# Up weights of an expert: column pieces of one pass in place of quarters of the rows

## The reference

```python
logits = t @ router_w + router_b              # 640 tokens x 32 experts
vals, idx = lax.top_k(logits, 4)              # 4 experts a token, softmax weights
def expert_block(e, toks, w):
    hh = t[toks] @ w_up[e] + b_up[e]          # w_up[e]: 1024 x 2048
    glu = minimum(hh[:, :1024], 7)
    lin = clip(hh[:, 1024:], -7, 7)
    y = (glu * sigmoid(1.702 * glu) * (lin + 1)) @ w_down[e] + b_down[e]   # 1024 x 1024
    return y * w
```

## Time and profile before

| | us |
|---|---|
| timed runs (three) | 1877.72, 1878.63, 1874.29; median 1877.72 |
| the profiled execution's own time | 1864.97 |
| its span, from the first to the last instruction | 1863.1 |
| PE busy with matmuls in the span | 1654.8 (89%) |
| DVE, ACT, POOL busy | 757.7, 342.3, 205.2 |

### The profile page before, as it was taken

The page is one execution under the profiler, slowest core; times in us unless marked ns, Lnnn a source line. Parts: engine busy times, 40 slices in busy tenths (PEclk is TensorE's granted clock), DMA queues, the critical chain, the costliest instruction groups (busy, mean ns, idle before and its releaser), DMA issues.

```text
span 1863.1 us, 52100 instructions
## 1 busy us (share of the span) xinstructions
PE 1654.8 (89%) x21067; PEld 988.3 (53%) x21068; DVE 757.7 (41%) x2254; ACT 342.3 (18%) x679; POOL 205.2 (11%) x274
## 2 busy tenths in 40 slices
PE   4999998987899873998998999999899998999967
PEld 2545456466675552655554565565455554555523
DVE  2432337346552666433333343334243333343317
ACT  0002211532010110221221222122122221122200
POOL 0000010200001210010110111011001100001026
PEclk9999999999899875998999999999999999999968
DMA  9634041920756256899889978998999999999994
GB/s 350 244 117 169 1 123 50 304 64 1 200 167 154 104 226 249 338 417 414 329 339 416 378 294 356 416 364 340 418 408 419 416 416 417 415 417 417 418 348 147
DMA packets 170599, 539.36 MB, mean 289 GB/s; under 512 B 24810, under 2 KB 75182, under 8 KB 137732
## 3 DMA queue, kind: packets, MB, share of 16 engines
q1 hardware_dynamic: 144080, 501.34, 69.5%
q0 software_dynamic: 7392, 22.81, 3.3%
q10 hardware_dynamic: 19028, 13.77, 2.4%
HBM read 502.57 MB, written 35.17 MB: 289 GB/s over the span
## 4 chain that ended last, share of the span: by engine, by line
PE 38%; DMA 16%; SPq 4%; DVE 1%; issue 1%; ACT 0%; POOLq 0%; POOL 0%; DVEq 0%
PE psum L1914 24%; DMA arena<-in_w_down 15%; PE psum L1922 12%; SPq L1825 3%; PE psum L1745 1%; DMA arena<-in_ln_b 1%; SPq L1830 1%; PE psum L1733 1%; SPq L1862 0%; DMA arena<-d_u,arena 0%; DVE arena L1782 0%; SPq L129 0%; DVE arena L1774 0%; SPq L131 0%; DVE arena L1776 0%
## 5 line engine op out<-in xcount | busy, mean ns | idle before, releaser
L1914 PE MATMUL psum<-arena 128*32 128x192 f32 (+1 forms) x11904 | 676.9, 385 | 53.4 <-issue 27.7
L1914 PEld LDWEIGHTS psum<-arena 128*32 128x32 f32 x11904 | 395.8, 111 | 330.7 <-issue 69.2
L1922 PE MATMUL psum<-arena 128*32 128x256 f32 x5952 | 343.3, 381 | 14.5 <-DMA arena<-in_w_down 14.5
L1975 DVE STREAM_TRANSPOSE arena<-psum 128x320 f32<-128x320 f32 (+1 forms) x186 | 83.7, 450 | 561.4 <-PE psum L1914 561.4
L1922 PEld LDWEIGHTS psum<-arena 128*32 128x32 f32 x5952 | 183.1, 110 | 147.0 <-DVE arena L1988 33.0
L1897 ACT ACT_TABLE_LOAD x93 | 119.3, 1283 | 259.8 <-issue 226.1
L1897 ACT ACTIVATE arena<-arena 128x160 f32<-128x160 f32 (+1 forms) x186 | 57.6, 310 | 401.4 <-DVE arena L1980 401.4
L428 PE MATMUL psum<-arena 128*128 128x512 f32 (+1 forms) x320 | 115.1, 521 | 0.6 <-DMA arena<-in_w_in 0.6
L1873 POOL COPY arena<-arena 128x1 uint32 (+1 forms) x94 | 17.1, 182 | 891.0 <-DVE arena L1969 852.7
L1876 POOL DMA_INDIRECT arena<-d_u,arena x94 | 92.1, 979 | 74.0 <-POOL arena L1873 74.0
L428 PEld LDWEIGHTS psum<-arena 128*128 128x128 f32 x320 | 56.9, 190 | 58.9 <-issue 57.3
(11 more groups left out here) (383 smaller groups left out, 1424.7 us busy)
## 6 DMA issues: line engine op xcount, KB each, us to landing
arena<-in_w_up SPq DMA_DIRECT2D x128, 2048.0 KB, 19.6
arena<-in_w_down SPq DMA_DIRECT2D x64, 2048.0 KB, 30.6
arena<-in_w_ada SPq DMA_DIRECT2D x10, 2048.0 KB, 19.4
d_y<-arena ACTq DMA_DIRECT2D x372, 32.0 KB, 5.8
arena<-in_w_in SPq DMA_DIRECT2D x5, 2048.0 KB, 7.7
d_y<-arena SPq DMA_DIRECT2D x1, 10240.0 KB, 33.0
arena<-in_cache_ckv SPq DMA_DIRECT2D x8, 1024.0 KB, 6.0
arena<-d_q SPq DMA_DIRECT2D x32, 144.0 KB, 3.4
```

The source lines that it names most:

```text
L1914: ins = pe.matmul(S[h][c * U:(c + 1) * U, 0:2 * U * (b1 - b0)].rearrange("p (g b j) -> p g b j", g=2, j=U), xT[:, 2 * q + k, :], up[par][q ...
L1922: ins = pe.matmul(Y[c * U:(c + 1) * U, 0:256], hidT[:, n, :], down[par][n // 4][:, n % 4, c * 256:(c + 1) * 256], start=(n == 0), stop=(n ...
L1975: dve.transpose(wide, S[h][:, 0:2 * U * w]).then_inc(s["h_turned"], 1)
```

## The change

w_up is cut in four pieces another way: by the columns of one pass and half of the rows. Pieces 0 and 1 are columns 0 to 639 of both halves g, rows 0 to 511 and 512 to 1023 (2.62 MB each); pieces 2 and 3 are columns 640 to 1023 of both halves, the same rows (1.57 MB each). The up pass goes through pieces 0, 1, 2, 3, waits for each at its own place and counts up_done after each; up_acc is dropped, and DVE waits for the second count of up_done in its place. A piece is read by two DMAs, one for each half g, whose runs of contiguous memory are 640 or 384 floats in place of 2048; a piece's semaphore then rises by 32. The sizes of the pieces ask for other addresses in the ring, and the first loads take the pieces in another order. w_down, the number of matmuls, their columns and the order over the rows within a pass stay as they are.

```diff
-RING_AT = [[43960, 48056, 15288, 11192, 19384, 23480], [31672, 27576, 3000, 7096, 35768, 39864]]
+RING_AT = [[43960, 11192, 49080, 16312, 19384, 23480], [27576, 3000, 32696, 8120, 35768, 39864]]
...
+def up_pieces(I):
+
+    rows = I["w_up"][0].rearrange("e (i k p) (g n) -> e i p k g n", i=2, p=P, g=2)
+    return [rows[:, i, :, :, :, b0 * P:b1 * P] for b0, b1 in PARTS for i in range(2)]
+
+
+def up_place(v, par, q):
+
+    b0, b1 = PARTS[q // 2]
+    return v.cut(RING_AT[par][q], 4, 2, P * (b1 - b0))
...
             def first(q):
-                sp.dma_start(v.cut(RING_AT[1][q], 2, 2 * FF), first_up(0, q)).then_inc(s["ring_in"][6 + q], 16)
-
-            first(0)
+                for g in range(2):
+                    sp.dma_start(up_place(v, 1, q)[:, :, g], w_up[q][0, :, :, g]).then_inc(s["ring_in"][6 + q], 16)
+
+            first(2)
             for t in range(NT):
                 if t == NT - 2:
                     sp.wait_ge(s["mT_acc"], 2 * NT)
-                    first(1)
+                    first(0)
                 if t == NT - 1:
                     sp.wait_ge(s["wo_acc"], NT)
-                    first(2)
+                    first(1)
                     first(3)
...
-            for q in range(3):
-                sp.dma_start(v.cut(RING_AT[0][q], 2, 2 * FF),
-                             w_up[bass.ds(long0, 1), :, q].rearrange("e p k n -> p (e k) n")
-                             ).then_inc(s["ring_in"][q], 16)
+            for q in (0, 2, 3):
+                for g in range(2):
+                    sp.dma_start(up_place(v, 0, q)[:, :, g], w_up[q][bass.ds(long0, 1), :, :, g].rearrange(
+                        "e p k n -> p (e k) n")).then_inc(s["ring_in"][q], 16)
...
             def load_up(e, par, q):
-                sp.dma_start(v.cut(RING_AT[par][q], 2, 2 * FF),
-                             w_up[bass.ds(e, 1), :, q].rearrange("e p k n -> p (e k) n")
-                             ).then_inc(s["ring_in"][6 * par + q], 16)
+                for g in range(2):
+                    sp.dma_start(up_place(v, par, q)[:, :, g], w_up[q][bass.ds(e, 1), :, :, g].rearrange(
+                        "e p k n -> p (e k) n")).then_inc(s["ring_in"][6 * par + q], 16)
...
-            load_up(long0, 0, 3)
+            load_up(long0, 0, 1)
...
-            def up_step(par, q, h):
-                b0, b1 = PARTS[h]
-                for k in range(2):
+            def up_step(par, q):
+                h, i = q // 2, q % 2
+                w = PARTS[h][1] - PARTS[h][0]
+                for k in range(4):
                     for c in range(C4):
-                        ins = pe.matmul(S[h][c * U:(c + 1) * U, 0:2 * U * (b1 - b0)
-                                             ].rearrange("p (g b j) -> p g b j", g=2, j=U),
-                                        xT[:, 2 * q + k, :], up[par][q][:, k, :, b0:b1, c, :],
-                                        start=(q == 0 and k == 0), stop=(q == 3 and k == 1))
+                        ins = pe.matmul(S[h][c * U:(c + 1) * U, 0:2 * U * w].rearrange("p (g b j) -> p g b j", g=2, j=U),
+                                        xT[:, 4 * i + k, :], up[par][q][:, k, :, :, c, :],
+                                        start=(i == 0 and k == 0), stop=(i == 1 and k == 3))
                 return ins
...
-                    pe.wait_ge(s["ring_in"][6 * par + g], times * 16 + RING_USED[6 * par + g])
+                    pe.wait_ge(s["ring_in"][6 * par + g], times * (32 if g < 4 else 16) + RING_USED[6 * par + g])
...
-                for h in range(NPART):
-                    for q in range(4):
-                        if h == 0:
-                            loaded(q)
-                        ins = up_step(par, q, h)
-                        if h == NPART - 1:
-                            ins.then_inc(s["up_done"], 1)
-                    if h < NPART - 1:
-                        ins.then_inc(s["up_acc"], 1)
+                for q in range(4):
+                    loaded(q)
+                    up_step(par, q).then_inc(s["up_done"], 1)
...
-                                dve.wait_ge(s["up_acc"], b * (NPART - 1) + (1 + h))
+                                dve.wait_ge(s["up_done"], b * 4 + 5)
```

More of the change, by code:

```diff
@@ L1374, in _ @@
             sp.dma_start(raw, I["b_up"][0].rearrange("e (q k p) -> (e q) k p", q=4, p=P)).then_inc(s["rw_in"], 16)
-            first_up = lambda e, q: I["w_up"][0, e].rearrange("(q k p) n -> q p k n", k=2, p=P)[q]
+            w_up = up_pieces(I)
             first_down = lambda e, h: I["w_down"][0, e].rearrange("(h n p) d -> h p n d", h=2, p=P)[h]
             def first(q):
-                sp.dma_start(v.cut(RING_AT[1][q], 2, 2 * FF), first_up(0, q)).then_inc(s["ring_in"][6 + q], 16)
-            first(0)
+                for g in range(2):
+                    sp.dma_start(up_place(v, 1, q)[:, :, g], w_up[q][0, :, :, g]).then_inc(s["ring_in"][6 + q], 16)
+            first(2)
             for t in range(NT):
@@ L1401, in _ @@
             long0 = sp.value_load(v.order[0:1, 0:1], min_val=0, max_val=NE - 1)
-            w_up = I["w_up"][0].rearrange("e (q k p) n -> e p q k n", k=2, p=P)
-            for q in range(3):
-                sp.dma_start(v.cut(RING_AT[0][q], 2, 2 * FF),
-                             w_up[bass.ds(long0, 1), :, q].rearrange("e p k n -> p (e k) n")
-                             ).then_inc(s["ring_in"][q], 16)
+            for q in (0, 2, 3):
+                for g in range(2):
+                    sp.dma_start(up_place(v, 0, q)[:, :, g], w_up[q][bass.ds(long0, 1), :, :, g].rearrange(
+                        "e p k n -> p (e k) n")).then_inc(s["ring_in"][q], 16)
         @block.scalar
@@ L1795, in stage_experts @@
     C4 = 4
-    up = [[v.cut(RING_AT[par][q], 2, 2, FF).rearrange("p k g (b c j) -> p k g b c j", b=KD, c=C4) for q in range(4)]
-          for par in range(2)]
+    up = [[v.cut(RING_AT[par][2 * h + i], 4, 2, P * (b1 - b0)).rearrange("p k g (b c j) -> p k g b c j", b=b1 - b0, c=C4)
+           for h, (b0, b1) in enumerate(PARTS) for i in range(2)] for par in range(2)]
     down = [[v.cut(RING_AT[par][4 + h], 4, D) for h in range(2)] for par in range(2)]
@@ L2025 @@
 top_neg ex_ready wts_ready hot_ready hot_acc sc2_ready mask_ready pos_acc order_ready idx_in idx_seen xg_in xT_ready bias_acc bias_set bias_sel
-up_acc up_done down_done h_turned h_sum h_clip h_cut h_prod sig_ready hid_ready
+up_done down_done h_turned h_sum h_clip h_cut h_prod sig_ready hid_ready
 y_ready y_out ohw_turned ohwT_ready f_in
```

## The result

The changed kernel takes 1905.8 us in the median of four runs (1899.22 to 1910.47) against 1877.76 of the kernel before (four runs): the medians lie 28.0 us (1.5%) apart. The ratio of the runs with its 95% interval is 1.0170 (1.0138 to 1.0201), which is 26 to 38 us. The profiled execution took 1904.67 us (span 1902.8).

A forecast was written before the change was run, and what follows sets the result against it. The prediction saw an expert stage bound by PE in its middle and by DMA elsewhere, above all from 1267 us on. Terms +2.8 and +26.8 make +29.6 us: 1877.7 + 29.6 = 1907 us, range 1884 to 1924 us.

The forecast's parts named there:

- Two regimes: Expert stage: with many tokens per expert transfers wait for PE; with two or three units left PE waits for transfers.
- the two busy runs: Expert stage, DMA busy throughout: three loads from 788.31 us, +2.8 us; 16 loads from 1267.45 us, +26.8 us.
- The price of a run: w_up loads: shorter contiguous runs make each expert's load 1.85 us longer, bounds 0 and 4.2 us.
- the line through four rates: Rates of 4 KB, 2 KB, 1 KB and 512 B rows give 37 ns per KB and about 9.5 ns per row.
- The release: Expert's last unit: the first transfer can start 2.80 us earlier, counted once in each of two DMA-busy stretches.
- Everything else at zero. PE: PE in the expert stage: 64 matmuls a unit, same columns in the same order of k, so no cost.
- Matmul means are unchanged: Sign that the forecast is right: the mean time of PE's matmuls stays as before.
- SP at zero: SP's queue: 8 issues for 4 per load, 0.65 us apart, cost nothing since SP waits 477.5 us for PE.
- Free runs: Rival for the stretch from 1267 us: short runs cost nothing, -5.6 us, 1872 us; chance 0.10.
- half the price: Rival on w_up loads: 0.85 us a load in place of 1.85, +10.6 us, 1888 us; chance 0.12.
- the price of the 1 KB row: Rival on w_up loads: short reads go like 1 KB rows, 4.2 us more a load, +74 us, 1952 us; chance 0.05.
- holes swallow the rest: Rival for the last DMA-busy stretch: PE sets the pace and DMA's idle time covers the price, about 1878 us; chance 0.05.

The follow-up runs named there:

- one factor: Changed kernel with each half of w_down also read by two transfers, so every weight semaphore rises by 32: 1.0150 to the kernel before.
- short runs alone: Kernel before, order and waits kept, each w_up quarter read by four transfers in runs of 640 or 384 floats: 1.0209 to the kernel before.
- order alone: Changed kernel with its pieces, order and issues, w_up read in contiguous runs of 10240 or 6144 B (weights land wrongly, timing only): 0.9992 to the kernel before.

## Why the prediction was right, and where it was not

**The bound.** Two regimes, with the price paid only where DMA is full: shown by the places of the loss, +2.0 and +25.4 us in the two busy runs against the forecast's +2.8 and +26.8. The holes between swallowed the loads of that part: with one factor the short runs leave units 14 to 50 at 393.4 us against 393.5. That the first run came within 1 us is in part luck, since kernels with long runs differ by 3.4 us there (161.3 to 164.7).

**The price of a run.** The cause is shown by the pair of short runs alone and order alone, with the gaps in memory left open. Its size: 1.85 us a load was forecast, from the line through four rates of earlier stages; 393 GB/s in the last run followed from it, and 396 was measured where the queue is full (390 in the window that was named, with 8 us of idle DMA in it). From these rates a load of 12.58 MB takes 12.58 / 396 less 12.58 / 416 = 1.53 us more. The table says much the same: three pairs of kernels that differ in their runs, over the 19 loads of the two busy runs, give 1.52 and 1.54 (order of after) and 1.76 us (order of before, with twice the issues). So the line was 5 to 20% too high for 2560 and 1536 B; for 4 KB runs of w_up it was too low, and for longer runs of w_down it promised too much. The rule of the Trainium skill quoted in the forecast ("DMA: Bandwidth & Descriptors", Specifications), by which such runs cost nothing, does not hold here: 396 and 394 against 416 GB/s.

**The release.** Its time is right (2.80 us), its worth is not settled: 5.6 us were subtracted, 2.4 measured by the ratio with 0 and 5.6 both inside, and the pairs of traces give 2.2 to 10.7. The two busy runs together lost 27.4 us where 29.6 were forecast. A price of 1.53 with a release of 2.4 makes 26.7, and one of 1.76 with a release of 6 makes 27.4: the runs do not tell these apart, so it stays open whether the release was too large as well as the price.

**The step that failed: "Everything else at zero. PE".** The columns and their order are indeed unchanged, but PE also executes the waits. Two factors for its semaphores cost 0.06 us a unit, some 3 us between the busy runs (396.8 against 393.4 us with one factor). That made up for the 2.2 us which the two terms above lacked, so the total, +29.6 against 30.6 in the stage and 28.0 in the medians, looks better than its terms: there luck has a part. "Matmul means are unchanged" failed too: behind the longer waits the granted clock was lower (0.61 in 1620 to 1623 us), and a down matmul took 388 in place of 381 ns. What of that lies on the path is not shown; transfers set the pace there.

**SP at zero** held for the time: issues in 8 KB runs doubled cost 0.0024, the second factor included. But "0.65 us apart" was wrong after an idle DMA: the first issue comes 2.56 us into the unit (2.1 was told), and the eight take 16 us. That nothing is lost by it is argued: SP stands there because the queue is full, so the transfers go on.

**The rivals.** Free runs would have been 1872 us and half the price 1888: both fall with 396 GB/s, as does the price of the 1 KB row. That holes swallow the rest falls with PE's waits for weights, 50.0 in place of 30.4 us (some 25 more were told, 19.6 came).

## What to carry to other kernels

Where a queue is full, price a re-cut of a transfer by its contiguous runs: fit rate against run length from saturated stretches of the same profile, and multiply by the transfers that no idle stretch follows. Then ask the reverse question, whether the layout could make runs longer, and put the step that this needs where it costs nothing, here in the matmul's write and not in its read; and look at the small transfers on other queues, which long runs can make late. When a semaphore's count per transfer changes, look at what the waiting engine has to compute for it in every pass of a loop.

## What the runs showed of the hardware that was not expected

- Weights in 16 KB runs on one queue made 32 KB writes on another land 9 to 10 us after their issue, with 5.8 before, and the kernel 2.6% slower though its weights came faster (425 GB/s from 1700 to 1760 us, 417 before).
- A second factor for the waits of one loop costs PE 0.06 us a unit (10.38 to 10.44 us) between two passes of full work.
- A moving operand read with a step of 20 bytes took 148 ns in place of 70 for 320 columns, with 12 bytes 68 in place of 44 for 192; a write to PSUM with a step of 128 bytes cost nothing (7.09 us a pass). The Trainium skill ("SBUF — State Buffer", section on the DMA port swizzle) lets fp32 step by up to four elements for free and calls any non-contiguous pattern in PSUM slow for matmuls; the read with 12 bytes (three elements) and the write contradict that. The same passage says that each access which crosses to a new 16-byte line pays, and most accesses with a step of 12 bytes do: by that sentence the slow read was to be expected.
- SP's eight issues behind an idle DMA took 16.22 us with runs of 2560 and 1536 B, 10.38 with 4 KB and 4.49 with 8 KB: with short runs the issuing engine stands sooner, and the page's chain names SPq where it named DMA.
